# Nine products of the unit matrix in the waits of TensorE around the router of a mixture of experts

## The chip, the cores and the metric

The kernel runs on one core of a Trainium2 chip. The metric is the device time of one execution in microseconds (us); the median of three executions is given. The profile is of one execution, taken by the hardware profiler. Its times are counted from the start of its span, which is the time from the first to the last instruction.

## What is computed

One layer of a hybrid encoder is computed for 512 prompt rows and 64 sample rows of 1024 numbers, all in 32-bit floats. First comes a normalization, one input projection and three kinds of mixers (band attention, gated linear attention, a state-space scan), then an output projection with residual. The change lies behind that, in the mixture of experts:

```python
def hier_moe(h, w_rg, b_rg, w_re, b_re, w_gate, w_up, w_down):
    hf = h.astype(F32)
    lg = hf @ w_rg.astype(F32) + b_rg.astype(F32)
    g_idx = jnp.argmax(lg, axis=-1)
    p_grp = jnp.take_along_axis(jax.nn.softmax(lg, axis=-1), g_idx[..., None], axis=-1)
    le = (hf @ w_re.astype(F32) + b_re.astype(F32)).reshape(bsz, L, N_EXPERT_GROUPS, EXPERTS_PER_GROUP)
    le = jnp.take_along_axis(le, g_idx[..., None, None], axis=2)[:, :, 0]
    top_v, top_i = lax.top_k(le, TOP_K_IN_GROUP)
    w_sel = jax.nn.softmax(top_v, axis=-1) * p_grp
    ...
    hid = jax.nn.silu(jnp.einsum('bld,edf->blef', h, w_gate)) * jnp.einsum('bld,edf->blef', h, w_up)
    hid = hid * gate.astype(h.dtype)[..., None]
    return jnp.einsum('blef,efd->bld', hid, w_down)
```

A row goes to the first group by its logits and to the two best of that group's four experts. There are 16 experts, each with two matrices of 1024 x 256 (gate and up) and one of 256 x 1024 (down): 3 MB each, 48 MB in all. A last normalization makes the output.

## The kernel before, in words

Each engine has its own program, written by hand in the order in which it runs, and the engines meet at semaphores. The 576 rows are handled in five tiles (four of 128 and one of 64). PSUM has eight banks. `fill(key, b)` lets TensorE wait until bank b was read by its last reader, and `done` says that the bank is full; `drained(eng, key)` waits for the reader, `filled` for the writer. `mm` is a matmul and `tr` a transpose (a product with the unit matrix `ident`).

What TensorE does from the end of the output projection on:

- For the last tile: the output projection (line 827, `out_proj_last`), two groups of transposes of the normalized rows `h2` (line 854), and the 20 router logits of each row (line 865). Between these it waits for VectorE and ScalarE.
- It then waits for `picks`. VectorE works out the router's choice in some 25 small steps (lines 2025 to 2050); its result `picked` holds a one for each row and chosen expert.
- "pos" (lines 896 and 897): 15 products of 16 columns in bf16 that count, for each row, the earlier rows of the same expert. "tot" (line 903): five more for the expert's whole count.
- VectorE turns "pos" into places (lines 2054 to 2060) and these into one-hot matrices (`mark_slots`, line 2072). `expert_ids(q)` on TensorE (line 917, five products of 3 columns) turns these into the list of rows of pass q, which VectorE writes to `router_index` (lines 2083 to 2086). `AHEAD` is 3: the lists of passes 0, 1 and 2 are made first.
- GpSimd gathers the rows of pass q from DRAM into `expert_x` (`gather(q)`, line 1257). Its order is: gather(0), gather(1), ten scattered writes of `slot_tokens` (line 1280), gather(2), gather(3), and from then on a gather and a scattered add of results (line 1267) in turns.
- ScalarE, in its order: `silu(0)` and `place_x(1)`, then, once all ten scattered writes have landed, nine small DMAs that read the weights of the slots (lines 1610 and 1614), then `silu(1)` (line 1569), `place_hidden(0)` (line 1575), `place_x(2)` (line 1582).
- The 12 passes of TensorE: `expert_in(q)` transposes the gathered rows (line 925), `expert_up(q)` multiplies them with gate and up (line 941, four column tiles of 32 rows side by side), `expert_turn(q)` transposes the hidden values (line 948) and `expert_down(q)` multiplies with down (line 962). Their order is: ids(3), up(0), in(1); then in each round ids(q+3), up(q), turn(q-1), in(q+1), down(q-1).
- SyncE loads the weights of later experts into buffers that `expert_up` or `expert_down` has given free (line 1021).

Of the kernel before, what the change touches and what calls it, by code (L numbers as in the profile page):

```python
# [28 lines left out]
def encoder_layer(nc, ins, outs):  # L29
# [8 lines left out]
    NT = SEQ // P + 1  # L38
# [9 lines left out]
    NE, _, FE = exp_gate.shape[1:]  # L48
# [30 lines left out]
    with ExitStack() as ctx:  # L79
        sems = {}  # L80

        def S(name):
            if name not in sems:
                sems[name] = ctx.enter_context(nc.semaphore(name))
            return sems[name]
# [16 lines left out]
        wring, _, _ = sb("weight_ring", [P, NSLOT, KD * SLOT_W])  # L102
        down, down_at, down_end = sb("down_ring", [P, 2, FE // P * D])
        ident, _, _ = sb("ident", [P, P])
        triu, _, _ = sb("triu", [P, P])
        striu, _, _ = sb("striu", [P, P])
        ones, _, _ = sb("ones", [P, P])
        par, _, _ = sb("params_T", [P, 64])
        small, _, _ = sb("small", [P, 256])
# [3 lines left out]
        cso, _, e = sb("conv_state_out", [4, 2, CH], at=mixT_at)  # L113
        sto, _, e = sb("ssd_state_out", [PC, 2, 2 * P], at=e)
        assert e <= mixT_at + 4 * WA // P * TOK
        iot, _, e = sb("iota", [P, 2, P], I32, at=mixT_at + 4 * WA // P * TOK)
        lvf, _, e = sb("level_compare", [P, 3, P], at=e)
        prow, _, e = sb("params_rows", [64, P], at=e)
        assert e <= mixT_at + 4 * KD * TOK
        stage, stage_at, _ = sb("stage", [P, 2, D])  # L120
        mixer_at = place[0]

        kB, _, _ = sb("gla_kT", [P, TOK])
        qB, _, _ = sb("gla_qT", [P, TOK])
        bcum, _, _ = sb("gla_b", [P, TOK])
        wup, _, _ = sb("gla_w_up", [RANK, HB * DK])
        qbd, _, _ = sb("gla_q_blocks", [P, HB, P])
        qE, qE_at, e = sb("gla_q_decayed", [P, 2, HB, P // 2], at=place[0])
        qk, _, e = sb("gla_qk", [P, P], at=e)
        hsel, _, e = sb("gla_head_of_row", [P, HB], at=e)  # L130
        place[0] = qE_at + 8 * HB * P
        assert e <= place[0]
        kE, _, _ = sb("gla_k_decayed", [P, 2, P])
        dif, _, _ = sb("gla_exponents", [P, 2, P])
        att, _, _ = sb("gla_scores", [P, HB, P])
        qs, _, _ = sb("gla_q_from_start", [P, P])
        kd, _, _ = sb("gla_k_to_end", [P, P])
        kdn, _, _ = sb("gla_k_to_end_nat", [P, P])
        Sg, _, _ = sb("gla_state", [P, 2, HB, DV])
        bv, _, _ = sb("gla_v", [P, NT, HB * DV])  # L140
        ogz, _, _ = sb("gates", [P, NT, HB * DV + HC * PC])
        lmask, _, _ = sb("level_masks", [P, 8, P], mybir.dt.uint8)
        gv, _, _ = sb("gla_o", [P, HB * DV])
        gt, _, _ = sb("gla_o_tmp", [P, HB * DV])

        xpre, _, e = sb("conv_in", [P, CH // P, TOK + 6], at=down_at)
        ctmp, _, e = sb("conv_sum", [P, 2, TOK + 4], at=e + (-e) % 32)
        thx, _, e = sb("conv_tanh", [P, TOK + 4], at=e + (-e) % 32)
# [3 lines left out]
        xnat, _, _ = sb("xB_nat", [P, 3 * P])  # L152
        dec, _, _ = sb("ssd_decay", [P, HC, P])
        cbm, _, _ = sb("ssd_cb", [P, 2, P])
        xdt, _, _ = sb("ssd_x_dt", [P, HC, PC])
        xw, _, _ = sb("ssd_x_w", [P, HC, PC])
        xD, _, _ = sb("ssd_x_skip", [P, HC, PC])
        hst, _, _ = sb("ssd_state", [P, 2, 2, PC])
        yv, _, _ = sb("ssd_y", [P, HC * PC])
        yt, _, _ = sb("ssd_tmp", [P, HC * PC])  # L160
        xc, xc_at, xc_end = sb("conv_out", [P, CH // P, TOK + 4])

        ckT, _, e = sb("att_cached_kT", [P, WA // P, PAST], at=xc_at)
        cv, _, e = sb("att_cached_v", [P, PAST // P, WA], at=e)
        assert e <= xc_end
        qT, qT_at, _ = sb("att_qT", [P, WA // P, TOK])
        kT, kT_at, kT_end = sb("att_kT", [P, WA // P, TOK])
        V, V_at, _ = sb("att_v", [P, NT, WA])
        gth, _, _ = sb("gates_tanh", [P, NT, 512], at=V_at)
        mixer_end = place[0]  # L170

        rtab, _, _ = sb("bias_table", [HA, 2 * CLIP + 1], at=qT_at)
        xrel, _, e = sb("bias_table_long", [HA, 384], at=qT_at + 1056)
        xlast, _, e = sb("x_last_tile", [P, D], at=e)
        assert e <= kT_at
        gtmp, _, e = sb("gla_tmp", [P, 2, TOK], at=kT_at)
        lrT, _, e = sb("gla_lowrank", [RANK, TOK], at=e)
        lrn, _, e = sb("gla_lowrank_nat", [P, NT, RANK], at=e)
        assert e <= kT_end

        knat, _, e = sb("att_k_nat", [P, NT, WA], at=hT_at)
        assert e <= hT_end
        bias, _, e = sb("att_bias", [P, HA, 2 * P], at=down_at)
# [3 lines left out]
        w2b, _, e = sb("norm2_b", [P, D], at=e)  # L187
        Pm, _, e = sb("att_p", [P, 2, 512], at=e)
        PT, _, e = sb("att_pT", [P, 2, 512], at=e)
        ye, _, e2 = sb("expert_y", [P, YBUF, D], at=x1_at)  # L190
        assert e2 <= e
        h2, h2_at, e = sb("h2", [P, 2, D], at=e)
        sg, _, e2 = sb("expert_silu", [P, 2, FE], at=h2_at)
        hid, _, e2 = sb("expert_hidden", [P, 2, FE], at=e2)
        hidT, _, e2 = sb("expert_hiddenT", [P, 2, FE // P, P], at=e2)
        assert e2 <= e
        lgt, _, e = sb("router_logits", [P, NT, NG + NE], at=e)
        ones_b, _, e = sb("ones_bf16", [P, P], BF16, at=e)
        before_b, _, e = sb("earlier_bf16", [P, P], BF16, at=e)
        tokid, _, e = sb("token_parts", [P, NT, 3], BF16, at=e)  # L200
        trash, _, e = sb("trash_row", [P, 2], at=e)
        idw, _, e = sb("token_and_weight", [P, NT, 2, 2], I32, at=e)
        wq, _, e = sb("slot_weight", [P, PASSES, 2], I32, at=e)
        more_id, _, e = sb("more_token_and_weight", [P, 2], I32, at=e)
# [200 lines left out]
        def drained(eng, key):  # L405

            b, _, n = fills[key]
            eng.wait_ge(S(f"bank{b}_free"), n)
# [15 lines left out]
        def _(pe):  # L424
# [11 lines left out]
            def done(ins, key):  # L436
                ins.then_inc(S(f"bank{fills[key][0]}_full"), 1)
# [430 lines left out]
            for n in range(HEADS):  # L868
                p, second = divmod(n, 2)
                if not second and p < NT * PAIRS:  # L870
                    scores(p)
                if not second and 1 <= p <= NT * PAIRS:
                    weigh(p - 1)
                if second and 1 <= p <= NT * PAIRS:
                    values(p - 1)
                for i, step in steps_behind(n):
                    if i == NT - 1:
                        if step in LAST_WO:
                            out_proj_last(*LAST_WO[step])
                    elif step in WO_PARTS:  # L880
                        out_proj(i, WO_PARTS[step])
                    if step in (12, 14):
                        turn_h2(i, (step - 12) // 2)
                    if step == 16:
                        logits(i)
                meanwhile(2 if n < 12 else 1)
                if n == 11:
                    meanwhile_until(("v", NT - 1))
                    spare[0] = (2, 2)
            pe.wait_ge(S("picks"), 1)  # L890

            o = fill("pos", 5)
# [8 lines left out]
            for i in range(NT):  # L901
                r = ROWS[i]
                last = mm(o[:, 0:NE], ones_b[0:r, :], picked[0:r, i, :], start=(i == 0), stop=(i == NT - 1))
            done(last, "tot")


            TILES = [slice(t * SHARE, (t + 1) * SHARE) for t in range(P // SHARE)]

            def expert_ids(q):

                if q >= PASSES:
                    return
                pe.wait_ge(S("slot_one_hot"), q + 1)
                o = fill(("ids", q), 4 + q % 2)
                for i in range(NT):
                    r = ROWS[i]
                    last = mm(o[:, 0:3], onehot[0:r, q % 2, i, :], tokid[0:r, i, :], start=(i == 0), stop=(i == NT - 1))
                done(last, ("ids", q))

            def expert_in(q):  # L920
                pe.wait_ge(S(f"xg{q % 2}_in"), 16 * (q // 2 + 1))
                for hf in range(2):
                    o = fill(("xgT", q, hf), hf)
                    for k in range(4):
                        last = tr(o[:, k * P:(k + 1) * P], xg[:, q % 2, (4 * hf + k) * P:(4 * hf + k + 1) * P], ident[:, :])  # L925
                    done(last, ("xgT", q, hf))
# [39 lines left out]
            for q in range(PASSES + 1):  # L966
                if q == 0:
                    for n in range(AHEAD):
                        expert_ids(n)
                    expert_in(0)  # L970
                if q == PASSES - 1:
                    expert_turn(q - 1)
                    expert_down(q - 1)
                    expert_up(q)
                    continue
                if q < PASSES:
                    expert_ids(q + AHEAD)
                    expert_up(q)
                if q >= 1:
                    expert_turn(q - 1)  # L980
                if q + 1 < PASSES:
                    expert_in(q + 1)
                if q >= 1:
                    expert_down(q - 1)
# [1225 lines left out]
```

## Time and profile before

| | us |
|---|---|
| median of 3 executions | 605.67 |
| lowest, highest | 605.45, 607.72 |
| the profiled execution, device time | 606.17 |
| its span | 604.4 |
| TensorE busy | 529.9 (88%) |
| VectorE, ScalarE, GpSimd busy | 260.1, 164.4, 107.6 |

The profiled execution took 606.17 us, its span is 604.4 us, so 1.77 us lie around the span. The granted clock is the share of its full speed that TensorE's clock was given; 1.0 stands for 2.4 GHz and 0.5 for 1.2 GHz. In the page's rows of 40 slices one slice is 15.1 us. In the chain of waits each piece released the next one.

### The profile page before, as it was taken

How to read it: one execution, taken by the hardware profiler on the slowest of the kernel's cores; microseconds unless marked ns; L12 is line 12 of the kernel's file. 1: busy time of each engine (PE TensorE's matmuls, PEld its weight loads, DVE VectorE, ACT ScalarE, POOL GpSimd, SP SyncE). 2: the span in 40 equal slices, each digit the busy share in tenths (PEclk: the TensorE clock that was granted, in tenths of full speed). 3: DMA queues.
4: the chain of work that ended last, by engine and by line, in shares of the span. 5: the costliest groups of instructions: out<-in, count | busy, mean ns of one | idle time of the engine just before them, and what ended most of it. 6: DMA issues, size and time to landing. Idle time of an engine off the chain costs nothing.

```text
span 604.4 us, 8597 instructions
## 1 busy us (share of the span) xinstructions
PE 529.9 (88%) x3186; PEld 297.3 (49%) x3186; DVE 260.1 (43%) x751; ACT 164.4 (27%) x438; POOL 107.6 (18%) x144
## 2 busy tenths in 40 slices
PE   1999999989999999989999999973699999999820
PEld 1777774545777775434555555542333333333200
DVE  1701265757676763533556555336423222211004
ACT  5302244243222323123444343210111121112103
POOL 4000001314141322200000000001632212221213
PEclk9899999999999999989999999985599999999985
DMA  7851206003002102236545020769279999999738
GB/s 238 298 169 59 81 1 210 0 2 139 1 2 76 65 1 65 95 111 232 184 153 204 1 106 36 296 232 324 58 235 337 348 350 338 345 362 331 175 59 305
DMA packets 63999, 100.03 MB, mean 166 GB/s; under 512 B 10365, under 2 KB 43312, under 8 KB 63926
## 3 DMA queue, kind: packets, MB, share of 16 engines
q1 hardware_dynamic: 53962, 78.26, 37.1%
q0 software_dynamic: 4448, 13.39, 9.0%
q10 hardware_dynamic: 5548, 7.83, 3.6%
q8 instruction: 26, 0.43, 0.3%
q14 instruction: 15, 0.12, 0.1%
HBM read 85.01 MB, written 17.08 MB: 169 GB/s over the span
## 4 chain that ended last, share of the span: by engine, by line
PE 50%; DVE 4%; issue 4%; DMA 3%; ACT 1%; POOL 1%; DVEq 0%; SPq 0%; POOLq 0%
PE bank L941 14%; PE bank L843 9%; PE bank L962 7%; PE bank L575 3%; PE bank L788 2%; PE bank L807 2%; PE bank L925 2%; PE bank L771 2%; PE bank L865 2%; PE bank L827 1%; DMA weight_ring<-x_rows 1%; DMA x_rows<-expert_y,router_index 1%; PE bank L854 1%; DMA expert_x<-h_rows,router_index 1%; PE bank L948 1%
## 5 line engine op out<-in xcount | busy, mean ns | idle before, releaser
L941 PE MATMUL bank<-weight_ring,expert_xT 128*32 128x512 f32 x336 | 79.8, 600 | 0.0
L941 PE MATMUL bank<-gate_up,expert_xT 128*32 128x512 f32 x432 | 72.8, 610 | 1.3 <-ACT expert_xT L1582 0.6
L560 PE MATMUL bank<-hT,weight_ring 128*128 128x288 f32 x256 | 69.9, 410 | 0.0
L843 PE MATMUL bank<-weight_ring,mixT 128*128 128x512 f32 x128 | 60.0, 602 | 0.0
L1188 POOL TENSOR_TENSOR small<-small 128x1 f32<-128x1 f32 (+5 forms) x25 | 18.6, 752 | 198.8 <-DVE small L1656 198.8
L560 PEld LDWEIGHTS bank<-hT,weight_ring 128*128 128x128 f32 x256 | 47.0, 190 | 10.9 <-issue 0.5
L463 PE MATMUL bank<-hT,weight_ring 128*128 128x288 f32 x192 | 49.3, 418 | 1.2 <-ACT gla_v L1359 0.9
L962 PE MATMUL bank<-down,expert_hiddenT 128*32 128x512 f32 x288 | 43.6, 595 | 2.2 <-issue 1.8
L463 PEld LDWEIGHTS bank<-hT,weight_ring 128*128 128x128 f32 x192 | 37.2, 195 | 12.3 <-issue 1.9
L941 PEld LDWEIGHTS bank<-gate_up,expert_xT 128*32 128x32 f32 x432 | 20.2, 112 | 36.4 <-issue 35.6
L2125 DVE TENSOR_TENSOR expert_hidden<-bank,expert_silu 128x256 f32<-128x256 f32 x12 | 5.1, 425 | 73.8 <-ACT expert_silu L1569 73.8
L575 PE MATMUL bank<-weight_ring,hT 128*128 128x512 f32 x64 | 33.1, 636 | 0.0
L843 PEld LDWEIGHTS bank<-weight_ring,mixT 128*128 128x128 f32 x128 | 22.5, 190 | 21.2 <-issue 20.6
L1215 POOL TENSOR_TENSOR gla_q_decayed<-gla_q_blocks,gla_exponents 128x256 f32<-128x256 f32 (+1 forms) x34 | 24.7, 732 | 42.9 <-issue 23.5
L1267 POOL DMA_INDIRECT x_rows<-expert_y,router_index x12 | 20.3, 1689 | 62.6 <-DVE router_index L2086 23.9
L1569 ACT ACTIVATE expert_silu<-bank 128x256 f32<-128x256 f32 x12 | 4.6, 384 | 98.1 <-PE bank L941 98.1
L546 PE MATMUL bank<-weight_ring,hT 128*128 128x512 f32 x64 | 30.4, 595 | 0.0
L941 PEld LDWEIGHTS bank<-weight_ring,expert_xT 128*32 128x32 f32 x336 | 20.0, 111 | 18.0 <-issue 17.9
L2142 DVE TENSOR_SCALAR expert_y<-bank,slot_weight 128x512 f32<-128x512 f32 x12 | 9.0, 750 | 39.3 <-PE bank L962 39.3
L645 PE MATMUL bank<-gla_q_decayed,gla_k_decayed 128*128 128x256 f32 (+1 forms) x68 | 19.9, 375 | 5.8 <-POOL gla_q_decayed L1215 5.3
L1985 DVE TENSOR_TENSOR bank<-bank,att_bias 128x256 f32<-128x256 f32 (+1 forms) x32 | 12.6, 394 | 26.9 <-PE bank L771 26.8
L1529 ACT ACTIVATE att_pT<-bank 128x128 f32<-128x128 f32 (+3 forms) x40 | 14.3, 400 | 33.4 <-PE bank L788 33.4
(329 smaller groups left out, 824.3 us busy)
## 6 DMA issues: line engine op xcount, KB each, us to landing
down<-in_exp_w_down SPq DMA_DIRECT2D x12, 1024.0 KB, 11.7
weight_ring<-in_w_in SPq DMA_DIRECT2D x5, 2048.0 KB, 9.2
gate_up<-in_exp_w_gate SPq DMA_DIRECT2D x18, 512.0 KB, 10.1
gate_up<-in_exp_w_up SPq DMA_DIRECT2D x18, 512.0 KB, 10.3
weight_ring<-in_exp_w_gate SPq DMA_DIRECT2D x14, 512.0 KB, 8.8
weight_ring<-in_exp_w_up SPq DMA_DIRECT2D x14, 512.0 KB, 10.0
weight_ring<-in_w_out SPq DMA_DIRECT2D x2, 2048.0 KB, 8.2
down_ring<-in_exp_w_down SPq DMA_DIRECT2D x4, 1024.0 KB, 11.3
```

The lines of the kernel that those rows point to most:

```text
L463: last = mm(bank[b][0:m, 0:HALF], w[:, k, c0:c0 + m], hT[:, k, half], start=(k == 0), stop=(k == KD - 1))
L546: last = mm(o[0:ROWS[i], :], hT[:, k, T0[i]:T0[i] + ROWS[i]], w[:, k, :], start=(k == 0), stop=(k == KD - 1))
L560: last = mm(o[:, 0:HALF], w[:, k, j * P:(j + 1) * P], hT[:, k, half], start=(k == 0), stop=(k == KD - 1))
L575: last = mm(o[0:ROWS[i], :], hT[:, k, T0[i]:T0[i] + ROWS[i]], w[:, k, :], start=(k == 0), stop=(k == KD - 1))
L645: last = mm(o[0:r, 0:HB * r // 2], kE[:, c % 2, 0:r], qE[:, c % 2, :, 0:r // 2], start=True, stop=True)
L843: last = mm(bank[3][0:ROWS[i], 0:512], mixT[:, k, T0[i]:T0[i] + ROWS[i]], ring(G_WO0 + hf, 512)[:, k, :], start=(k == 0), stop=(k == KD - 1))
L941: last = mm(o[t, :], xgT[:, q % 2, k, t], w[:, k], start=(k == 0), stop=(k == KD - 1))
L962: last = mm(o[t, :], hidT[:, q % 2, j, t], w[:, j * D + hf * 512:j * D + (hf + 1) * 512], start=(j == 0), stop=(j == FE // P - 1))
L1188: g.tensor_tensor(small[0:rows, out:out + n], small[0:rows, col:col + n], small[0:rows, A_MH:A_MH + n], ALU.pow).then_inc(S(sem), 1)
L1215: g.tensor_tensor(qE[:, c % 2, :, 0:r // 2].rearrange("p h (n m) -> p h n m", m=m), later(qbd[:, :, 0:r], m), e_.unsqueeze(1).broadcast_to ...
L1267: g.indirect_dma_start(out=x1_d, out_offset=index, in_=ye[:, q % YBUF, :], in_offset=None, compute_op=ALU.add).then_inc(S("y_added"), 16)
L1529: free(a(PT[:, h, 0:nb * r], src[:, 0:nb * r], ACT.Copy), ("PT", p - 1, h))
```

## The change

TensorE's program gets a function `keep_busy(n)` that issues n products of `ident` (128 x 128) with `w2b`, the row of norm weights in 32-bit floats, 512 columns wide. They write bank 3, whose reader has finished before, and nobody reads them. It is called three times: with 4 between the last logits and the wait for `picks`, with 1 behind "tot", and with 4 behind `expert_ids(2)`, ahead of `expert_in(0)`. Nothing else is changed; the programs of the other engines have the same rows.

```diff
+            def keep_busy(n):
+
+                for _ in range(n):
+                    mm(bank[3][:, 0:512], ident[:, :], w2b[:, 0:512], start=True, stop=True)
+
+            drained(pe, ("wo", NT - 1, 0))
+            keep_busy(4)
             pe.wait_ge(S("picks"), 1)
...
             done(last, "tot")
+            keep_busy(1)
...
                     for n in range(AHEAD):
                         expert_ids(n)
+                    keep_busy(4)
                     expert_in(0)
```

TensorE's order before, from the last logits to the first rows of `expert_up(0)` (L897 and L896 are "pos", L903 is "tot", L917 x15 are the three lists of rows, L925 is `expert_in(0)`):

```order
L865 MATMUL bank<-router_w,h2T 64x20 x8
L897 MATMUL bank<-picked,earlier_bf_124 128x16
...
L897 MATMUL bank<-picked,earlier_bf_124 64x16
L903 MATMUL bank<-picked,ones_bf_123 128x16 x5
L917 MATMUL bank<-token_parts,slot_one_hot 128x3 x15
L925 MATMUL bank<-ident,expert_x 128x128 x8
L917 MATMUL bank<-token_parts,slot_one_hot 128x3 x5
```

The same stretch in the changed kernel, whose line numbers are 7 or 8 higher from there on (L904 and L903 are "pos" there, L910 is "tot", L925 the lists, L933 `expert_in(0)`; L893 is `keep_busy`):

```order
L865 MATMUL bank<-router_w,h2T 64x20 x8
L893 MATMUL bank<-norm_b,ident 128x512 x4
L904 MATMUL bank<-picked,earlier_bf_124 128x16
...
L904 MATMUL bank<-picked,earlier_bf_124 64x16
L910 MATMUL bank<-picked,ones_bf_123 128x16 x5
L893 MATMUL bank<-norm_b,ident 128x512
L925 MATMUL bank<-token_parts,slot_one_hot 128x3 x15
L893 MATMUL bank<-norm_b,ident 128x512 x4
L933 MATMUL bank<-ident,expert_x 128x128 x8
```

Nine products were put into the row at three places; nothing else changed its place.

## Rows read from the trace of the kernel before

**Rows 1.** The page: the span, and TensorE's granted clock in 40 slices.

```profile
span 604.4 us, 8597 instructions
...
PEclk9899999999999999989999999985599999999985
```

**Rows 2.** Windows: stretch, its us, busy us (x instructions) by engine, PEclk, DMA share, GB/s.

```profile
264.50:264.60 0.10, 0.10 (x2) 0.00 (x0) 0.00 (x0) 0.00 (x0) 0.00 (x0) 0.83 0.00 0
...
404.40:404.60 0.20, 0.20 (x3) 0.20 (x3) 0.00 (x0) 0.00 (x0) 0.00 (x0) 0.70 1.09 384
...
435.00:436.00 1.00, 1.00 (x16) 0.37 (x12) 0.00 (x0) 0.00 (x0) 0.70 (x2) 0.90 0.01 0
```

**Rows 3.** Timeline of TensorE, long products: start us, us, engine, line, xcount (records).

```profile
261.94 3.17 PE L575 MATMUL bank<-weight_ring,hT 128*128 128x512 f32 x4
...
435.50 0.61 PE L941 MATMUL bank<-gate_up,expert_xT 128*32 128x512 f32 x3
...
435.93 0.61 PE L941 MATMUL bank<-gate_up,expert_xT 128*32 128x512 f32 x3
```

**Rows 4.** Timeline, router: idle time before each in brackets, with its releaser.

```profile
411.10 1.87 PE L865 MATMUL bank<-router_w,h2T 128*64 128x20 f32 x16 [0.61 <-DVE h2T L2008]
...
418.10 0.19 PE L897 MATMUL bank<-picked,earlier_bf 128*128 128x16 bf16 x1 [5.13 <-DVE picked L2050]
...
421.04 0.38 PE L917 MATMUL bank<-token_parts,slot_one_hot 128*128 128x3 bf16 x5 [1.71 <-DVE slot_one_hot L2072]
...
423.21 0.38 PE L917 MATMUL bank<-token_parts,slot_one_hot 128*128 128x3 bf16 x5 [0.99 <-DVE slot_one_hot L2072]
```

**Rows 5.** The chain that ended last, 394 to 451 us: start us, us, what.

```profile
394.69 6.01 PE bank L827 x28
...
427.90 1.97 PE bank L925 x8
...
430.70 9.28 PE bank L941 x64
439.98 0.60 PE bank L925 x4
...
441.83 7.07 PE bank L941 x64
448.91 0.37 PE bank L948 x2
449.27 0.87 PE bank L925 x8
450.15 3.57 PE bank L962 x32
```

**Rows 6.** Timeline of GpSimd and ScalarE behind the router (q at an engine's name: DMA issue).

```profile
439.60 0.90 POOL L1280 DMA_INDIRECT slot_tokens<-token_and_weight,router_index  x1 [0.30 <-issue]
...
440.80 1.04 POOL L1257 DMA_INDIRECT expert_x<-h_rows,router_index  x1 [0.30 <-issue]
...
447.23 1.09 ACTq L1614 DMA_DIRECT2D slot_weight<-slot_tokens  x2
...
449.31 0.39 ACT L1575 ACTIVATE expert_hiddenT<-bank 128x256 f32<-128x256 f32 x1
```

**Rows 7.** Issue to landing: the scattered write at 439.6 us.

```profile
DMA to landing us min/median/max: 4.3/4.3/4.3
```

**Rows 8.** DMA issues by line: the ten scattered writes, median us to landing.

```profile
slot_tokens<-token_and_weight,router_index POOLq DMA_INDIRECT x10, 2.1
```

**Rows 9.** Issue to landing: the gather issued at 440.8 us.

```profile
DMA to landing us min/median/max: 7.2/7.2/7.2
```

**Rows 10.** The last two loads of `down` (engine op xcount, ns, starts), their landing, and TensorE's wait.

```profile
L1021 SPq DMA_DIRECT2D down<-in_exp_w_down x2: 432/572/711, 550.0 to 550.6; - x2
...
DMA to landing us min/median/max: 13.8/14.8/15.8
...
563.99 3.64 PE L962 MATMUL bank<-down,expert_hiddenT 128*32 128x512 f32 x32 [1.76 <-issue]
```

## The prediction

> **What bounds the kernel now.** I first read the slices of the page: TensorE's granted clock is 8 or 9 nearly everywhere, and 5 in two slices, with 8 and 5 at the very end [rows 1]. These two slices are the router. The windows give the edges: the clock fell to half near 404.5 and came back near 435.2 (0.90 is the mean of the microsecond from 435.0, so 0.2 us of it at half) [rows 2]. What did the engine do before? Before the fall, its last 512-column products had ended at 400.7 [rows 5]; then only short transposes and 20-column products ran. Before the rise, `expert_up(0)` had run 512-column products from 430.7 on: 4.5 us. An earlier rise, at 264.5, came 2.6 us after such products had begun [rows 2, 3]. So a rise costs 2.6 to 4.5 us of long products in the two cases shown.
>
> The timeline of the router [rows 4] shows TensorE waiting for others: it finishes the last logits at 412.97, idles 5.13 us until `picks`, idles 1.71 us before ids(0) (so "pos" and "tot" together took 418.10 to 419.33), and finishes ids(2) at 423.59. The chain [rows 5] has `expert_in(0)` at 427.90, after gather(0), and from there TensorE works nearly without a gap. Half clock is on the path there: 427.90 to 430.70 from `expert_in(0)` to `expert_up(0)`, where the next round has 1.85 us (439.98 to 441.83), and 9.28 us for `expert_up(0)` where the next has 7.07.
>
> Third, what stands close behind TensorE. GpSimd issues its last scattered write at 439.60, and gather(2) at 440.80, each 0.30 us after the one before, so it waits for no other engine [rows 6]. The write lands 4.3 us later, at 443.9 [rows 7]; ScalarE then issues nine DMAs, the last two until 448.32 [rows 6], and only then runs `silu(1)`. gather(2) lands 7.2 us after its issue, at 448.0 [rows 9].
>
> **The price of a product.** A 32-bit product of 512 columns makes two records. Groups of `expert_up` at full clock start 0.43 us apart [rows 3], so a product is 2 x 0.43 = 0.86 us at full and 1.72 us at half clock. Nine are 7.7 to 15.5 us of TensorE's time, all of it put where it idles.
>
> **First four.** They start at 412.97, with the clock at half. All four need 6.88 us at half clock, and the wait lasts 5.13. If the clock rises x us after the start, they end at 412.97 + x/2 + 3.44; x of 2.6 to 4.5 gives 417.7 to 418.7. "pos" could begin at 418.10, so it is delayed by 0 to 0.6 us. Against that, "pos" and "tot" took 1.23 us at half clock; "pos" is 15 of these 20 products, about 0.9 us (an estimate), of which full clock saves between nothing and half, 0.45. Call d the shift of everything behind "pos": -0.45 to +0.6, and I take 0, since the two ends come from the same unknown x. Queued behind this wait are "pos", the places, the lists, and so gather(0) and GpSimd's whole row: all shift by d.
>
> **The fifth.** 0.86 us (1.72 at half clock) in an idle of 1.71: nothing.
>
> **Last four.** They start behind ids(2), at 423.59 + d. With the clock still at full they end at 427.0, ahead of the rows' arrival at 427.9: hidden. But from the first block's end to here only 0.86 us of long products lie in 5 us, and the one fall shown came 3.8 us after the last of them. If the clock fell, these four take 4.7 to 5.7 us by the same formula and end at 428.3 to 429.3. So `expert_in(0)` starts 0 to 1.4 us late; I take 0.7 (428.6), the middle, since the fall is likely but the ramp's length is open.
>
> **What that gives at expert_up(0).** 428.6 + 1.85 + 7.0 (7.07 of the next round less its tail) = 437.45, against 439.98: 2.5 us earlier. Bounds: 427.9 gives 3.2 us; 429.3 + 0.6 gives 1.2. `expert_up(1)` then ends at 446.4 rather than 448.91.
>
> **What is late next.** Here most of the gain stops, as neither GpSimd nor ScalarE gets earlier than d. ScalarE is issuing until 448.32. `silu(1)` can start at 448.34 rather than 448.96, so `place_hidden(0)`, at 449.31 with 0.39 us in the row [rows 6], ends at 449.70 - 0.62 = 449.08, and `expert_down(0)`, which needs it, starts at 449.1 rather than 450.15 [rows 5]: 1.0 us earlier. The gather: `expert_in(2)` can start at 448.0 rather than 449.27, 1.3 us earlier [rows 5, 9]. The later gate counts. Net gain = 1.0 - d = 1.0 us, with 0.4 to 1.45 from d alone.
>
> Both gates depend on landings beside the weights' loads, which `expert_up(0)` releases. The ten scattered writes have a median of 2.1 us, the last one 4.3 [rows 7, 8]. If both landings were 2.2 us shorter, the gates would open at 446.9 and 445.8 and the gain of 2.5 would pass whole. If the write took as long as the gather (7.2 instead of 4.3), the gate would be 2.9 us later and the result -1.0 + 2.9 = 1.9 us slower. I take them unchanged: the last write already ran beside loads that were released at 440.0. The Trainium skill (Trainium Kernel Development and Optimization, Key Constraints) says that DMAs issued from SyncE, ScalarE and GpSimd all run on the same 16 engines and interleave. By that rule, loads that start 2.5 us sooner lie beside more of the scattered writes, which speaks against this change and for the 1.9 us slower; the pair 2.1 and 4.3 agrees in kind, and no row shows the size at the new time.
>
> **To the end.** Behind `expert_down(0)` the same round repeats in the chain, each piece starting where the one before it ends, so a shift passes through. One place can eat it: before 563.99 TensorE idled 1.76 us for the last `down` loads, issued at 550.0 and 550.6 and landing 13.8 to 15.8 us later [rows 10]. The loads must move too. Their queue is released by TensorE's passes, which move by 1.0, so I let it pass; if it did not, the gain would be 0.
>
> **Sum.** 604.4 - 1.0 = 603.4 of span, with 1.77 around it 605.2 for the profiled execution. That one lies 0.5 above the median of 605.67; against the median the forecast is 604.7.
>
> **The rivals.**
>
> - Forecast, the two gates hold: gain 0.4 to 1.6, 604.1 to 605.3. Chance 0.58.
> - The gates give way: the landings get shorter, as the weights' loads are over sooner, and 1.7 to 3.2 us pass: 602.5 to 604.0, middle 603.2. For it: 2.1 against 4.3 us [rows 7, 8]. Against: the loads still overlap. Chance 0.15.
> - Nothing comes through, for the loads at 550 do not move: 605.7. For it: a wait of 1.76 us that no engine's work ends [rows 10]. Against: the loads are released by TensorE. Chance 0.14.
> - The scattered writes are held up by the earlier loads: up to 1.9 slower, 607.6. Chance 0.05.
> - The change doesn't do what it says: products with the unit matrix don't lift the clock, or it rises only after them. The point from which it decides is a rise later than 6.88 us after 412.97. Then "pos" waits until 419.85, 1.75 late; the last four start at 425.3 and end at 432.2; `expert_in(0)` is 4.3 us late. If the clock comes at the old time, 435.2, `expert_up(0)` ends near 442.0, 2.0 late: 607.7. If the ramp starts anew, all 4.3 us stay: 610.0. For it: the rises shown came with real data, and x has only two cases. Against: both are well below 6.88. Chance 0.08.
>
> **How the numbers follow.** About 0.5%, or 3.0 us, is what a measurement of this kernel can tell from no change. Faster by over 3.0 takes the top of the second case alone: 0.05. Slower by over 3.0 takes the end of the last case, and the spread of three executions, whose highest lay 2.05 above the median: 0.05. The rest is 0.90. The range reaches from the middle of the second case, with a little of what is beyond (602.9), over the forecast and the third case to the spread above it (606.8); it leaves out the two slower cases and the top of the second.
>
> **What the changed profile would show.** The granted clock rises between 415.5 and 418.2; "pos" starts between 418.0 and 418.8. A second fall, if any, lies between 420 and 425, and a second rise before 429. `expert_in(0)` starts at 427.9 to 429.3 at full clock, with eight transposes in about 0.9 us, and `expert_up(0)` takes 7.0 us and ends near 437.5. A new wait of 1 to 2 us stands before `expert_in(2)` or `expert_down(0)`, released by the gather or by ScalarE, whose `silu(1)` follows its last DMA issue at once. The wait near 563 stays at 1.2 to 1.8 us. The prediction is wrong if the clock is still at half when "pos" runs, if the new wait is missing, or if the wait near 563 grows by what was gained.

## The result and the profile after

| | before | after |
|---|---|---|
| median of 12 executions, us | 605.69 | 611.36 |
| lowest, highest, us | 604.60, 607.91 | 604.48, 612.81 |
| profiled execution, us | 606.17 | 611.59 |
| its span, us | 604.4 | 609.8 |

The ratio on record is 1.0086, with a 95% interval of 1.0064 to 1.0108 (it is not the quotient of the two medians, which is 1.0094). The changed kernel is slower by about 0.9%. The forecast was 604.7 us, in a range of 602.9 to 606.8, and the result lies outside it. Ten of the twelve executions after lie between 610.31 and 612.81.

The page's span and granted clock in 40 slices, which answer to [rows 1]:

```profile
span 609.8 us, 8633 instructions
...
PEclk9999999999999999979999999987979999999975
```

The two slices at 5 are gone, so the router did run warmer. But there is a dip to 7 behind it, in the slice from 442 to 457 us, where before there was none. Windows of after, with the columns of [rows 2] (stretch, its us, busy us by engine PE, PEld, DVE, ACT, POOL, granted clock, DMA share, GB/s), give the levels:

```profile
412.40:416.90 4.50, 4.50 (x6) 1.92 (x7) 3.81 (x22) 0.22 (x1) 1.81 (x1) 0.50 1.08 385
417.20:418.20 1.00, 1.00 (x3) 0.29 (x2) 0.24 (x1) 0.00 (x0) 0.00 (x0) 1.00 1.08 383
424.00:427.20 3.20, 3.20 (x5) 1.35 (x4) 2.89 (x15) 0.00 (x0) 1.43 (x2) 0.50 0.54 142
427.50:428.60 1.10, 1.10 (x4) 0.44 (x3) 0.49 (x5) 0.00 (x0) 0.53 (x1) 1.00 0.61 231
...
451.30:452.30 1.00, 0.00 (x0) 0.00 (x0) 0.19 (x1) 0.61 (x3) 0.00 (x0) 0.50 1.10 356
452.40:458.00 5.60, 5.60 (x28) 1.39 (x32) 0.73 (x2) 0.84 (x2) 0.00 (x0) 0.50 0.74 204
458.20:458.70 0.50, 0.50 (x8) 0.00 (x0) 0.00 (x0) 0.09 (x1) 0.00 (x0) 1.00 0.00 0
```

The clock rises at 417.1, falls again at 423.9, and is back at 427.3: the warm-up works. Then it is at half from 451.2 to 458.1, with TensorE idle at the start of that stretch. The timeline of TensorE shows what stood there (start us, us, engine, line, operation, records, idle time before it and its releaser; L893 is `keep_busy`, L933 `expert_in`, L970 `expert_down`):

```profile
412.32 6.05 PE L893 MATMUL bank<-norm_b,ident 128*128 128x512 f32 x8
418.21 0.17 PE L904 MATMUL bank<-picked,earlier_bf 128*128 128x16 bf16 x1
...
423.46 5.40 PE L893 MATMUL bank<-norm_b,ident 128*128 128x512 f32 x8
428.70 1.04 PE L933 MATMUL bank<-ident,expert_x 128*128 128x128 f32 x8
...
437.57 1.09 PE L933 MATMUL bank<-ident,expert_x 128*128 128x128 f32 x8
...
447.54 1.09 PE L933 MATMUL bank<-ident,expert_x 128*128 128x128 f32 x8 [0.60 <-DMA expert_x<-h_rows,router_index]
452.40 1.08 PE L970 MATMUL bank<-down_ring,expert_hiddenT 128*32 128x512 f32 x3 [3.78 <-ACT expert_hiddenT L1584]
```

`expert_up(0)` ends just before the `expert_in(1)` at 437.57, where before it ended at 439.98 [rows 5]: 2.4 us earlier on the clock of the trace. But `expert_down(0)` begins at 452.40, where before it began at 450.15. A wait of 3.78 us for ScalarE stands ahead of it. The chain of waits, from the last scattered write on, says why (start us, us, what):

```profile
439.56 6.27 DMA slot_tokens<-token_and_weight,router_index
...
445.85 0.36 ACTq L1619
446.20 0.04 issue
446.24 1.45 ACTq L1623
...
451.69 0.10 ACT expert_silu L1578
451.79 0.18 issue
451.97 0.39 ACT expert_hiddenT L1584
452.36 0.04 issue
452.40 6.42 PE bank L970 x32
458.82 0.29 PE bank L925 x5
459.12 7.00 PE bank L949 x64
```

GpSimd issues the last scattered write at the old time (439.60 before [rows 6]), but it lands after 6.27 us instead of 4.3 [rows 7]. ScalarE's nine DMA issues then take from 445.85 to 451.64, 5.8 us instead of 4.45. Then `silu(1)` and `place_hidden(0)` run, and `expert_down(0)` starts at half clock and takes 6.42 us instead of 3.57 [rows 5]. `expert_up(2)` begins at 459.12, where in the chain of before it was at 454.01: 5.1 us late.

One thing has to be known before two traces are laid side by side: the router doesn't begin at the same time in both. VectorE reads the last logits here, in before and then in after:

```profile
413.00 0.17 DVE L2012 TENSOR_TENSOR router_logits<-bank,router_b 64x20 f32<-64x20 f32 x1 [2.05 <-PE bank L865]
```

```profile
412.43 0.17 DVE L2021 TENSOR_TENSOR router_logits<-bank,router_b 64x20 f32<-64x20 f32 x1 [2.05 <-PE bank L865]
```

After is 0.57 us ahead at this point, before any added product has run. From there to the last scattered write it takes 26.60 us before and 27.13 after. So GpSimd's row did not stay: it is 0.53 us later behind the router, and the earlier router hides it.

What changed around the scattered write is what the loads did. The loads that `expert_up(0)` releases are issued from 437.69 on, where before they were from 440.04. The DMA share from the last scattered write to its landing, in a window of before and then in one of after:

```profile
439.60:443.87 4.27, 3.63 (x37) 1.98 (x37) 2.42 (x7) 0.98 (x2) 2.95 (x3) 1.00 0.57 162
```

```profile
439.56:445.85 6.29, 6.29 (x60) 2.29 (x64) 1.13 (x5) 0.00 (x0) 2.94 (x3) 1.00 0.95 307
```

The share rose from 0.57 to 0.95, as the write now lies wholly beside the loads. My theory after this result: the warm-up's gain sets the loads free sooner, they hold up the write, ScalarE stands in line with `expert_hiddenT` behind nine DMA issues, and TensorE's wait then costs a second time, through its clock. The rivals: the last four products do harm by themselves; the clock fall is an accident beside the loss; or the loss lies in the loads' row to the end.

### The profile page after: what moved, and what is told of

It is laid out like the page before. It is cut to its first block, busy times and chain, and to the rows that moved or that the text cites. A ratio compares the mean times of both kernels' runs of the same rounds, so it can differ in the third digit from the quotient of the medians.

```text
span 609.8 us, 8633 instructions
## 1 busy us (share of the span) xinstructions
PE 540.7 (89%) x3204; PEld 300.5 (49%) x3204; DVE 261.2 (43%) x751; ACT 164.3 (27%) x438; POOL 108.5 (18%) x144
## 4 chain that ended last, share of the span: by engine, by line
PE 49%; DMA 3%; DVE 3%; issue 3%; POOL 2%; ACTq 1%; ACT 1%; DVEq 0%; SPq 0%; POOLq 0%
PE bank L949 11%; PE bank L843 9%; PE bank L970 8%; PE bank L575 5%; PE bank L788 2%; PE bank L807 2%; PE bank L771 2%; PE bank L865 1%; PE bank L933 1%; DMA weight_ring<-x_rows 1%; POOL slot_tokens L1289 1%; PE bank L827 1%; DMA slot_tokens<-token_and_weight,router_index 1%; DMA x_rows<-expert_y,router_index 1%; PE bank L893 1%
## 5 line engine op out<-in xcount | busy, mean ns | idle before, releaser
L949 PE MATMUL bank<-weight_ring,expert_xT 128*32 128x512 f32 x336 | 77.6, 593 | 0.0
L949 PE MATMUL bank<-gate_up,expert_xT 128*32 128x512 f32 x432 | 70.6, 593 | 1.3 <-ACT expert_xT L1591 1.3
L560 PE MATMUL bank<-hT,weight_ring 128*128 128x288 f32 x256 | 69.9, 410 | 0.0
L463 PE MATMUL bank<-hT,weight_ring 128*128 128x288 f32 x192 | 47.6, 408 | 1.3 <-ACT gla_v L1368 0.9
L970 PE MATMUL bank<-down,expert_hiddenT 128*32 128x512 f32 x288 | 46.4, 606 | 1.6 <-ACT expert_hiddenT L1584 1.6
## 6 DMA issues: line engine op xcount, KB each, us to landing
gate_up<-in_exp_w_up SPq DMA_DIRECT2D x18, 512.0 KB, 10.6
```

Source lines behind the costliest of these rows:

```text
L463: last = mm(bank[b][0:m, 0:HALF], w[:, k, c0:c0 + m], hT[:, k, half], start=(k == 0), stop=(k == KD - 1))
L560: last = mm(o[:, 0:HALF], w[:, k, j * P:(j + 1) * P], hT[:, k, half], start=(k == 0), stop=(k == KD - 1))
L949: last = mm(o[t, :], xgT[:, q % 2, k, t], w[:, k], start=(k == 0), stop=(k == KD - 1))
L970: last = mm(o[t, :], hidT[:, q % 2, j, t], w[:, j * D + hf * 512:j * D + (hf + 1) * 512], start=(j == 0), stop=(j == FE // P - 1))
```

## The experiments

Each run's median stands with its ratio to the kernel before on the same chip. The runs went to several chips, and the median of the kernel before was 605.69 beside after, 606.10 beside e1 to e4, 605.90 beside e5 to e8 and 605.34 beside e9 to e11. So the distance of two runs from each other is taken from their distances to the kernel before: after lies 5.7 us above it. The router's start moves by a few us from one execution to the next, so where two profiles are compared I also count from the last scattered write's issue to the first record of `expert_down(0)` in the timeline: 10.5 us before (439.60 to 450.08), 12.8 after (439.56 to 452.40). This count leaves out the 0.53 us by which the write itself is late. A profile shows one execution, and not always a typical one: those of e4, e9 and e11 are the longest of their run, those of e5 and e7 the shortest, and that of e2 took 617.90 us, where the other twelve took 609.22 to 613.89.

### ScalarE's order: e1_act_first and e2_before_act_first

The nine DMA issues go behind `silu(1)` and `place_hidden(0)`, in the kernel after (e1) and in the kernel before (e2):

```diff
-                place_x(q + 1)
-                place_y(q - 1)
-                if q == 0:
+                if q == 1:
                     act.wait_ge(S("map_written"), 16 * 2 * NT)
...
+                place_x(q + 1)
+                place_y(q - 1)
```

> The changed kernel, with ScalarE's nine small DMAs for the slot weights put behind silu(1) and place_hidden(0) instead of ahead of them. Theory (the loads released earlier hold up the last scattered write, ScalarE stands behind it and issues slowly, expert_down(0) waits for ScalarE, and in that wait the clock falls): ScalarE is off the path, the next gate is gather(2) at 447.5 instead of 449.3, expert_down(0) starts near 448.5 at full clock, and the time is 1.7 us below the kernel before, 603 to 605. Rival (the loss is the products' own, or the earlier loads slow everything): no better than 609.

> The kernel before with the same reordering on ScalarE alone. Theory: ScalarE was done issuing at 448.3 and waited for TensorE then, so it costs and gives nothing: within 0.5 us of the kernel before. Rival (the reordering helps by itself): 1 us or more below it.

Measured: e1 607.79 us, 1.0015 [0.9993, 1.0038]; e2 610.34 us, 1.0067 [1.0043, 1.0091]. In e1 `expert_down(0)` starts at 449.17, at full clock, 9.7 us behind the last write. So ScalarE's row was the gate, and most of the loss is gone. The expected 603 to 605 did not come, and ScalarE's timeline in e1 shows the next gate:

```profile
451.24 1.24 ACTq L1621 DMA_DIRECT2D slot_weight<-slot_tokens  x2
452.52 0.60 ACT L1591 ACTIVATE expert_xT<-bank 128x512 f32<-128x512 f32 x1 [5.29 <-issue]
460.48 0.69 ACT L1602 ACTIVATE expert_y<-bank,slot_weight 128x512 f32<-128x512 f32 x1 [7.36 <-DMA slot_weight<-slot_tokens]
```

The slot weights arrive only at 460.46. VectorE waits with `expert_y` in front of a list of rows, and TensorE waits 1.70 us for that list at 461.95.

e2 was a miss: I expected no change. My edit put `place_x(2)` behind the nine issues too. With the old times that stands in TensorE's way, as ScalarE's and then TensorE's timeline of e2 show:

```profile
455.57 1.22 ACTq L1612 DMA_DIRECT2D slot_weight<-slot_tokens  x2
456.84 0.60 ACT L1582 ACTIVATE expert_xT<-bank 128x512 f32<-128x512 f32 x1 [6.72 <-issue]
```

```profile
457.49 5.35 PE L941 MATMUL bank<-weight_ring,expert_xT 128*32 128x512 f32 x24 [3.05 <-ACT expert_xT L1582]
```

TensorE waited 3.05 us, and the clock was at half from 456.5 to 463.3. In this execution it is the picture of after, made in the kernel before without a single added product: a wait for ScalarE and a half-clock stretch. The median stands 4.2 us above the kernel before. Whether the typical execution of e2 has the half-clock stretch too isn't shown: the profiled one is the longest, with a mean granted clock of 0.942, and the others have 0.947 to 0.955, where the kernel before has 0.950 to 0.957.

### The loads: e3_hold_loads and e8_before_hold

SyncE holds the loads that `expert_up(0)` releases until the scattered writes have landed, in after (e3) and in before (e8):

```diff
                 if q < PASSES:
                     filled(sp, ("gu", q))
+                if q == 0:
+                    sp.wait_ge(S("map_written"), 16 * 2 * NT)
```

> The changed kernel; SyncE waits for the ten scattered writes to land before it issues the loads that expert_up(0) has released. Theory: the last write lands in 2 to 3 us rather than 6.3, ScalarE is done issuing near 446.5, silu(1) runs at once, no second wait of 4 us, no fall of the clock; 603 to 605, if the weights still come in time. Rival (the early loads are not the cause): 611 as the changed kernel.

> The kernel before with the loads released by expert_up(0) held until the scattered writes have landed. Theory: the last write lands in about 2 us instead of 4.3, the loads go out about 2 us later than at 440.0, nothing changes near 450, and the wait near 563 for the last down loads grows by about the same 2 us: 607.5. Rival (the loads have slack, the write was what mattered): 605.7 or below.

Measured: e3 607.71 us, 1.0022 [0.9998, 1.0046]; e8 605.78 us, 1.0000 [0.9983, 1.0018]. The landing in a window of e3:

```profile
438.40:440.43 2.03, 2.03 (x20) 0.73 (x24) 1.15 (x5) 0.00 (x0) 1.72 (x2) 1.00 0.02 1
```

With a DMA share of 0.02 the last write lands 2.0 us after its issue; with 0.57 it was 4.3, with 0.95 it was 6.3. That is the first half of the theory. The thirteen profiles together show the same. The first column is when the first load that `expert_up(0)` released was issued, counted from the issue of the last write:

| profiles | loads begin, us | DMA share until the landing | landing, us |
|---|---|---|---|
| e3, e8 (loads held) | 2.1 later | 0.02 | 2.0 |
| e2 | 0.7 later | 0.28 | 2.4 |
| before | 0.4 later | 0.57 | 4.3 |
| e5 | 0.1 sooner | 0.76 | 5.3 |
| e9, e7 | 0.4, 0.5 sooner | 0.87, 0.88 | 6.0, 6.1 |
| after, e1, e4, e10, e11 | 1.9 sooner | 0.94 to 0.98 | 6.3 to 6.5 |
| e6 | 2.1 sooner | 1.06 | 5.7 |

The landing grows as the loads come nearer, and from about half a microsecond ahead of the write on it grows little more. The kernel before stood on the steep part of this. Only the two ends are tested by an edit (e3, e8 against after, before); the rows between are what the other profiles happen to show, and e6, with the largest share and a shorter landing, is out of line. The Trainium skill (Trainium Kernel Development and Optimization, Key Constraints) says that DMAs of SyncE, ScalarE and GpSimd run on the same 16 engines and interleave; these three landings agree with it, and give it a size that it doesn't state. In e3 `expert_down(0)` begins 9.0 us behind the last write, 1.5 less than before. But the time is not below that of before, and the profile shows where the gain goes: weights come late near the end. TensorE's timeline of e3:

```profile
447.40 0.63 PE L970 MATMUL bank<-down_ring,expert_hiddenT 128*32 128x512 f32 x3 [0.74 <-ACT expert_hiddenT L1586]
...
558.56 0.63 PE L970 MATMUL bank<-down_ring,expert_hiddenT 128*32 128x512 f32 x3 [2.96 <-issue]
...
564.74 3.64 PE L970 MATMUL bank<-down,expert_hiddenT 128*32 128x512 f32 x32 [0.47 <-ACT expert_hiddenT L1586]
```

The wait of 2.96 us is one for weights, and the clock was at half from 559.2 to 562.6 behind it, so that `expert_down(9)` took 5.34 us and not 3.57. e8 was a miss: I expected 1.9 us of loss, and there was none; its wait for weights near the end is 1.60 us, not more than the 1.76 of before [rows 10]. So at the kernel before's pace the loads have that time to spare. That they don't in e3 because TensorE is earlier there is read from the two profiles, not tested.

### The clock fall alone: e4_warm_wait

Four more products, into a bank that is free, stand in the wait before `expert_down(0)`:

```diff
+                if q == 1:
+                    drained(pe, ("ids", 3))
+                    for _ in range(4):
+                        mm(bank[5][:, 0:512], ident[:, :], w2b[:, 0:512], start=True, stop=True)
```

> The changed kernel with four more products that nobody reads (bank 5) in the wait before expert_down(0). Theory: the wait stays, expert_down(0) still starts near 452.4, but at full clock with 3.6 us instead of 6.4: 2.8 us below the changed kernel, near 608.5. Rival (the fall of the clock there is chance or costs nothing): 611.

Measured: 608.19 us, 1.0019 [0.9998, 1.0040]. TensorE's timeline of e4:

```profile
448.72 1.09 PE L933 MATMUL bank<-ident,expert_x 128*128 128x128 f32 x8 [0.58 <-DMA expert_x<-h_rows,router_index]
449.65 3.60 PE L995 MATMUL bank<-norm_b,ident 128*128 128x512 f32 x8
453.73 0.63 PE L970 MATMUL bank<-down_ring,expert_hiddenT 128*32 128x512 f32 x3 [0.49 <-ACT expert_hiddenT L1588]
```

`expert_down(0)` is as late as in after (13.0 us behind the last write, against 12.8), but the clock stays at full and it takes 3.64 us. The median is 2.1 us above the kernel before, where that of after is 5.7 above it: 3.6 us less. Between the traces the difference of `expert_down(0)` is 2.8. So this wait costs TensorE about 2.3 us by itself and some 3 us more through the clock.

### One part alone: e5_first_four and e6_last_four

e5 keeps only the first four products, e6 only the last four; the other calls get 0.

```diff
-            keep_busy(1)
+            keep_busy(0)
...
-                    keep_busy(4)
+                    keep_busy(0)
```

```diff
-            keep_busy(4)
+            keep_busy(0)
...
-            keep_busy(1)
+            keep_busy(0)
```

> The kernel before with the first four products alone. Theory (what costs is that expert_up(0) ends early and so releases the loads early): the clock rises near 417 but falls again by 425, expert_up(0) runs at half clock as before and ends near 440, the loads go out at the old time: 605.0 to 606.5. Rival (the delay or the work of the first block costs): 608 or more.

> The kernel before with the last four products alone. Theory: they run 5 to 6 us across a rise, expert_in(0) starts near 428.5 at full clock, expert_up(0) ends near 437.5, and everything behind it is as in the changed kernel: 610 to 612. Rival (the loss comes from the first block): 605 to 606.

Measured: e5 605.57 us, 1.0001 [0.9983, 1.0018]; e6 609.43 us, 1.0066 [1.0047, 1.0085]. In e5 the clock was at half again from 418.2 to 431.9, `expert_up(0)` began at half clock, and `expert_down(0)` came 10.6 us behind the last write, as before. TensorE's timeline of e6:

```profile
421.34 5.18 PE L893 MATMUL bank<-norm_b,ident 128*128 128x512 f32 x8
...
449.03 1.07 PE L970 MATMUL bank<-down_ring,expert_hiddenT 128*32 128x512 f32 x3 [3.05 <-ACT expert_hiddenT L1584]
```

The wait for ScalarE was 3.05 us, and the clock was at half from 448.2 to 455.1. The last four alone cost 3.5 us, where all nine cost 5.7 (0.66% and 0.86%; the two intervals overlap). They do so by what they speed up: in e4 and e1 the same products stand in their place, and the time is 3.6 and 4.0 us lower. The profiles hold a source for the rest. From the last logits to `expert_down(0)` it takes 37.1 us before, 38.2 in e6 and 40.0 in after. Of the 1.7 us between e6 and after, 0.5 are the later scattered write, which only profiles with the first four show, 0.5 its longer landing (6.29 instead of 5.75) and 0.7 the nine issues (5.8 instead of 5.1). The first four alone (e5) cost nothing that the medians show.

### Another queue for the slot weights: e7_slots_sync and e11_sync_sooner

The same nine DMAs (`slot_weight<-slot_tokens`) are issued by SyncE: in e7 behind the loads that `expert_up(1)` releases, in e11 ahead of those, behind the ones that `expert_up(0)` releases.

```diff
                     if gu_after.get(e) == q:
                         load_gate_up(e)
+                if q == 1:
+                    sp.wait_ge(S("map_written"), 16 * 2 * NT)
...
+                        sp.dma_start(dst[0:CAP, :, j, :], own).then_inc(S("slot_weight_in"), 16)
```

> The changed kernel with the nine slot-weight DMAs issued by SyncE, behind the loads that expert_up(1) releases, instead of by ScalarE. Theory: ScalarE no longer stands in front of expert_down(0), which starts near 448.5 after the gather; the slot weights land by 460, before they are needed; the early loads keep the weights in time. 604 to 605.5. Rival (the weights' stream is the bound at the end whatever happens here, or the slot weights come late as when ScalarE issued them later): 607 or more.

> As e7_slots_sync, but SyncE reads the slot weights as soon as the scattered writes have landed, ahead of the loads that expert_up(1) releases. Theory: the slot weights land 4 us sooner, so the wait of 1.5 us near 458 goes; the loads behind go out up to 3.5 us later, and the wait for the last weights grows by a part of it: 604.5 to 607. Rival (the loads have slack of that size): 604 or less, faster than both kernels.

Measured: e7 606.50 us, 1.0015 [1.0001, 1.0028]; e11 608.73 us, 1.0052 [1.0028, 1.0076]. In e7 `expert_down(0)` comes 9.6 us behind the last write at full clock, but VectorE's timeline and then TensorE's show the slot weights late, as in e1:

```profile
458.10 0.75 DVE L2151 TENSOR_SCALAR expert_y<-bank,slot_weight 128x512 f32<-128x512 f32 x1 [10.15 <-DMA slot_weight<-slot_tokens]
```

```profile
459.56 0.41 PE L956 MATMUL bank<-ident,expert_hidden 128*128 128x128 f32 x2 [1.48 <-DVE router_index L2095]
```

In e11 the slot weights came in time, and it was the loads behind them that were late: issued from 451.78 on, 4.4 us after `expert_up(1)` had ended, where e7 issues them at once (446.03). TensorE's timeline of e11:

```profile
561.30 0.63 PE L970 MATMUL bank<-down_ring,expert_hiddenT 128*32 128x512 f32 x3 [3.22 <-issue]
```

Half clock followed from 561.9 to 565.3, as in e3.

### Is the end the floor? e9_before_skip and e10_sync_skip

The last three loads of `down` (experts 12, 13 and 14) are left out, in before (e9) and in e7 (e10); the last passes multiply by older weights, so part of the result is not computed.

```diff
-                    pe.wait_ge(S(f"down{s}_in"), 16 * n)
+                    pe.wait_ge(S(f"down{s}_in"), 16 * (n - (e in LOADS[-3:])))
...
+                if e in LOADS[-3:]:
+                    return
```

> The kernel before without its last three loads of down (experts 12, 13, 14; the last passes multiply with older weights, so part of the result is left out). It measures what the wait for the last weights costs. Theory (the end of the weights' stream is a floor under whatever is gained near 450): the wait of 1.8 us before pass 10's expert_down goes, 1.3 us of it shows: 604.0 to 604.6. Rival (that wait was for something else): no change.

> The kernel with the nine products and the slot weights read through SyncE (e7_slots_sync), without the same three loads. Theory: freed from the floor, the earlier start of expert_down(0) comes through less the wait of 1.5 us for the slot weights and plus nothing at the end: 1 to 2 us below e9_before_skip, 602.5 to 603.5. Rival (the gain is lost elsewhere, not at the last weights): as e9_before_skip or above, 604 to 606.

Measured: e9 605.13 us, 0.9996 [0.9980, 1.0013]; e10 604.41 us, 0.9989 [0.9972, 1.0007]. Neither reached what was expected. The late wait for weights is gone from both profiles (0.47 us for ScalarE is left), and yet nothing measurable is gained. The two differ by 0.7 us, not by 1 to 2; e10 still waits 0.62 us for `router_index` behind the slot weights. So the last weights alone are not the floor. The profile of e9 holds another answer, in TensorE's timeline:

```profile
450.29 0.63 PE L962 MATMUL bank<-down_ring,expert_hiddenT 128*32 128x512 f32 x3 [1.85 <-ACT expert_hiddenT L1577]
```

In that execution the clock came back at 432.9, not at 435.2, with none of the products added. `expert_up(0)` ended at 438.2, the last write took 6.0 us to land, and `expert_down(0)` came 11.6 us behind it. So in this one execution the program of before loses what an early clock gives it, by the same collision. It is the longest of its run (606.04); whether the others do the same isn't shown.

## Why the prediction was wrong, step by step

- **First four, d = 0: wrong by half a microsecond, and hidden by luck.** They ran from 412.32, and the clock rose 4.8 us later, where 2.6 to 4.5 was allowed for. `picked` was written at 417.46, and "pos" began only at 418.21. GpSimd's last write then came 27.13 us behind the last logits, before 26.60: d was +0.5, near the end of its own bounds, and by the prediction's "1.0 - d" half of the gain was gone with it. The two writes stand at 439.56 and 439.60 in their traces because the router began 0.57 us earlier in after. The other profiles bear this out: without the first four the same stretch took 26.6 us in all five (before, e2, e6, e8, e9), with them 27.0 to 27.7 in seven of eight, and 26.5 in e7, where the clock rose after 3.0 us. In these eight profiles the rise came 3.0 to 5.9 us after the start, 4.6 or more in seven.
- **The fifth: right.** Its 1.13 us lie in the idle time.
- **Last four: right.** The clock fell at 423.9 and rose at 427.3; `expert_in(0)` began at 428.70, forecast 428.6, and took 1.04 us. Counted from the last logits, this and the next time are about 0.6 us later than forecast; that they fit to a tenth is the same luck.
- **`expert_up(0)`: right in kind.** It ended at 437.5, forecast 437.45.
- **"I take them unchanged": the step that failed.** With both landings at their old size, `expert_down(0)` should have begun at 449.1; it began at 452.40, 3.3 us later. Of these, 2.0 are the landing (6.3 instead of 4.3), and 1.3 are the nine issues (5.8 instead of 4.45). The reason given, that the last write "already ran beside loads that were released at 440.0", was false in size: only the part behind 440.04 lay beside them, and the write lies wholly beside them now. e3 shows the price without them: 2.0. The gather, whose landing was to be the second gate, nearly kept its size: 6.7 us instead of 7.2 [rows 9], and it held `expert_in(2)` until 447.54, forecast 448.0.
- **The rival with 0.05 was the right mechanism**, and its text had the rule and the row for it. It was too small: it priced the landing by the gather (7.2, so 1.9 us slower) and left out both that ScalarE's issues might lengthen and that TensorE's wait might cost its clock.
- **A term was missing: +2.85 us.** The clock fell within the wait of 3.78 us, at 451.2, and was at half until 458.1. I had priced every added product against the clock, but not the idle time that a late gate would make. e4 measured this term by itself: 3.6 us in the medians, 2.8 between the traces.
- **To the end: passed through, as forecast.** From the end of `expert_down(0)` to the start of the `down` products behind the late wait took 110.27 us before and 109.59 after, so 0.7 us were given back: the late wait is one for ScalarE now (1.09 us), no longer for weights (1.76 [rows 10]). The rest took 40.4 us before and 41.4 after. Of this last 1.0, 0.74 is one read behind the passes (`weight_ring<-x_rows`, 7.34 against 6.60), which took between 6.66 and 7.85 in the profiles of e1 and e3 to e8, with or without the added products; nothing ties it to the change.

The sum, made again with what was measured: 603.4 + 3.3 + 2.85 - 0.7 + 1.0 = 609.85, and the span was 609.8. It was fitted to this trace and proves nothing beyond it. Counted from the last logits, `expert_down(0)` is 2.9 us later than before: d 0.5, landing 2.0 and issues 1.35, less the 1.0 of slack that the forecast took for its gain; the router's earlier start takes 0.57 off again.

**Shown**: that the loads set the landing (e3, e8 and the table), that ScalarE's order carries it to TensorE (e1, e7), that the clock adds some 3 us (e4), and that the last four alone set it off (e5, e6). **Read from the profiles, not tested by a run of its own**: the half microsecond of the first four. **Open**: why the nine issues take longer. They took 4.45 us before at a DMA share of 1.06, 5.8 in after at 1.01, and 6.2 in e3 at 0.83, so the share doesn't order them. In before SyncE issued nothing meanwhile, in after and e3 it did; no run tells this apart from other causes. Open too is why two executions of after took 604.48 and 608.39; neither was profiled. Their mean granted clocks were 0.966 and 0.964, where the other ten had 0.956 to 0.962. A stretch of 6.8 us at half clock is worth 0.006 in this mean, so it fits that they went without the late fall, as e4 does (0.962 to 0.967); that isn't shown. And no complete kernel beat the one before: e8, e5 and e7 come nearest, with ratios of 1.0000, 1.0001 and 1.0015.

## What to carry to other kernels

Warming TensorE in a wait did speed up the next stage nearly as computed, and made the kernel slower. A faster stage releases its buffers sooner: list the transfers that start with that, and ask which small transfer somebody waits for will now share the DMA engines with them. A queue in order that mixes DMA issues behind a semaphore with work on the path turns a late landing into a late engine. And price each new wait of TensorE twice, as idle time and as a possible clock fall.

## What the runs showed of the hardware

- A small scattered write of GpSimd landed in 2.0 us at a mean DMA share of 0.02 until its landing, and in 4.3 and 6.3 us at 0.57 and 0.95. It went with when the loads began: a start 0.7 us behind the write's issue gave 2.4 us, one 0.4 us ahead of it 6.0.
- Products of the unit matrix, mostly zeros, lifted the granted clock from 1.2 to 2.4 GHz: 4.8 us after their start in after, 3.0 in e6 and e7, 5.9 at most (e11). With real data, in `expert_up(0)`, it rose after 4.5 us in before and 3.3 in e9.
- Late waits of TensorE of 2.96 (e3), 3.05 (e2, e6), 3.22 (e11), 3.34 (e2) and 3.78 us (after) each came with a stretch at half clock, which began within the wait or less than 1 us behind it; with waits of 1.85 (e9) and 1.76 us (before) there was none. The stretches were of two lengths: 3.4 us in e3, e11 and the later one of e2, 6.8 us in after, e6 and the earlier one of e2. The Trainium skill (TensorE: Matmul & The Clock Gate, What's actually happening) says that for modeling the ramp's penalty is below 1% of a typical kernel's span. One fall here cost about 3 us of 606, 0.5%, which agrees; but that is half of the whole effect of this change, so it can't be left out of a sum of this size.
